# Masking the blocks that were not chosen: from bf16 products on TensorE to an addition on GpSimd

## The reference

```python
imp = jnp.einsum('bgrsc,cj->bsgj', p_cmp, overlap_matrix(ncmp, n_slc))
score = jnp.where(causal[:, None, :], jnp.where(forced[:, None, :], FORCE, imp), NEG)
_, idx = lax.top_k(score, topn)                       # 8 blocks per query and group
...
scs = jnp.einsum('bqgrd,bqgkd->bqgrk', qb, kg).astype(jnp.float32) * scale
scs = scs - slopes[None, None, :, :, None] * dist.astype(jnp.float32)
p = jax.nn.softmax(jnp.where(dist >= 0, scs, NEG), axis=-1)
return jnp.einsum('bqgrk,bqgkd->bqgrd', p.astype(vg.dtype), vg)
```

## Time and profile before

| what | value |
|---|---|
| median of 3 runs | 872.6 us (870.66 to 873.0) |
| span of the profiled execution, first to last instruction | 867.2 us |
| median less span | 5.4 us |
| TensorE / VectorE / ScalarE / GpSimd busy | 91% / 66% / 49% / 13% |
| `nsa_phase`, first to last instruction | 540.45 to about 762 us |
| mean granted TensorE clock | 0.961 |

### The profile page before, as it was taken

The page is one execution under the profiler, slowest core; times in us unless marked ns, Lnnn a source line. Parts: engine busy times, 40 slices in busy tenths (PEclk is TensorE's granted clock), DMA queues, the critical chain, the costliest instruction groups (busy, mean ns, idle before and its releaser), DMA issues. The chain is left out here.

```text
span 867.2 us, 16180 instructions
## 1 busy us (share of the span) xinstructions
PE 786.8 (91%) x6290; PEld 664.0 (77%) x6290; DVE 571.2 (66%) x1334; ACT 426.7 (49%) x966; POOL 113.7 (13%) x61
## 2 busy tenths in 40 slices
PE   4899999996988889877989998989998999989996
PEld 4899987685777767756868887778877888878885
DVE  6961111035789899847755997899998988943332
ACT  5631111113556565626743322778888888822221
POOL 0000000002000000002105421123110332132220
PEclk9999999998999999969998999899999999989999
DMA  7220125243232323134134431500001111034421
GB/s 293 103 86 38 37 98 154 77 112 111 67 104 68 104 67 98 55 92 134 49 87 137 122 86 41 146 2 1 3 2 51 50 51 50 2 122 146 146 98 48
DMA packets 31788, 72.34 MB, mean 83 GB/s; under 512 B 5088, under 2 KB 13664, under 8 KB 30688
## 3 DMA queue, kind: packets, MB, share of 16 engines
q1 hardware_dynamic: 31712, 71.31, 26.8%
HBM read 55.04 MB, written 16.25 MB: 82 GB/s over the span
## 5 line engine op out<-in xcount | busy, mean ns | idle before, releaser
L1645 ACT ACTIVATE n_probs<-n_probs,n_negated_max 128x640 f32<-128x640 f32 (+7 forms) x128 | 94.2, 736 | 28.4 <-DVE n_negated_max L1714 28.1
L1723 DVE SCALAR_TENSOR_TENSOR n_probsT_low<-n_turned,n_probsT_high 128x512 f16<-128x512 f32 (+3 forms) x192 | 94.4, 520 | 16.8 <-ACT n_probsT_high L1655 14.1
L706 PE MATMUL n_turned<-identity,n_probs 128*128 128x128 f32 x528 | 82.9, 281 | 6.3 <-ACT n_probs L1645 4.3
L1655 ACT ACTIVATE n_probsT_high<-n_turned 128x512 f16<-128x512 f32 (+3 forms) x192 | 80.7, 454 | 12.2 <-PE n_turned L706 11.8
L1817 PE MATMUL n_scores<-w_and_keys_high,stacks 128*128 128x256 f32 (+2 forms) x192 | 75.2, 392 | 5.5 <-DVE n_negated_max L1714 3.4
L706 PEld LDWEIGHTS n_turned<-identity,n_probs 128*128 128x128 f32 x528 | 59.6, 142 | 24.1 <-ACT n_probs L1645 16.4
L1818 PE MATMUL n_scores<-w_and_keys_low,stacks 128*128 128x256 f32 (+2 forms) x192 | 61.9, 333 | 0.0
L620 PE MATMUL nat<-stacks,xT_high 128*128 128x256 f32 (+1 forms) x192 | 56.1, 292 | 2.3 <-issue 2.2
L621 PE MATMUL nat<-stacks,xT_high 128*128 128x256 f32 (+1 forms) x192 | 55.2, 287 | 0.0
L622 PE MATMUL nat<-stacks,xT_low 128*128 128x256 f32 (+1 forms) x192 | 55.1, 287 | 0.0
L180 PE MATMUL a_projected<-xT_high,w_and_keys_high 128*128 128x512 f32 x128 | 52.3, 409 | 0.7 <-ACT staged L189 0.7
(11 more groups left out here) (263 smaller groups left out, 2177.3 us busy)
## 6 DMA issues: line engine op xcount, KB each, us to landing
w_raw<-in_w_feat SPq DMA_DIRECT2D x23, 512.0 KB, 3.9
features<-staged SPq DMA_DIRECT2D x30, 256.0 KB, 2.5
a_raw<-features SPq DMA_DIRECT2D x36, 128.0 KB, 2.7
s_raw<-features SPq DMA_DIRECT2D x18, 256.0 KB, 4.1
branches_b_c<-in_x SPq DMA_DIRECT2D x8, 512.0 KB, 6.2
silu_gates<-staged SPq DMA_DIRECT2D x16, 256.0 KB, 2.0
gatesT<-silu_gates SPq DMA_DIRECT2D x8, 512.0 KB, 4.8
keys_and_w_out_raw<-in_w_out SPq DMA_DIRECT2D x4, 1024.0 KB, 5.2
```

What stands on the lines that cost most here:

```text
L706: mm = nc.tensor.transpose(dst[:, j, :], src[:, c:c + P], ident[:, :])
L1645: nc.scalar.activation(pr[:, n % PS, 0:w], pr[:, n % PS, 0:w], ACT.Exp, scale=-1.0, bias=nmax[:, hb % 4, qt:qt + 1], accum_out=sums[:, hb ...
L1655: nc.scalar.activation(pth[:, g % GS, 0:k, :], tp[g % TS][:, 0:k, :], ACT.Copy, scale=PSCALE).then_inc(t_high, 1)
L1723: nc.vector.scalar_tensor_tensor(out=ptl[:, g % GS, 0:k, :], in0=tp[g % TS][:, 0:k, :], scalar=PSCALE, in1=pth[:, g % GS, 0:k, :], op0=ALU ...
```

## The change

The mask is no longer a product. `choose` writes -1e30 itself for a block that was not chosen (else 0), into a table `unsel` that outlives `cmp_phase`. In `nsa_phase` GpSimd adds it, each entry broadcast over the 64 keys of its block, to the distance table, once for each of the two head groups and four query tiles, into a new table `mb` of 3328 columns; the masked `add_bias` reads `mb` instead of `bf`. Gone are: the transposes and the cast at the end of `cmp_phase`, the memset of the old table, the load of `blocks` (512 KB) and its cast, the 64 products of L1822 (two for each of 32 masked units), and the wait of `a_squares` for the cast.

```diff
@@ choose, on VectorE in cmp_phase
-                nc.vector.tensor_tensor(unsel[:, g, :, 0:NSLC], left[:, :, :], imp[:, :, :],
-                                        ALU.is_equal).then_inc(chosen, 1)
-                dve.wait_ge(chosen, g + 1)
+                ch.link(nc.vector.tensor_scalar(unsel[:, g, :, :], left[:, :, :], -BIG / 2, NEG, ALU.is_gt, ALU.mult))
...
@@ ScalarE and TensorE at the end of cmp_phase
-            act.wait_ge(chosen_turned, 1)
-            nc.scalar.copy(unselT[:, :, :], tp[0][:, 0:KV, :]).then_inc(mask_ready, 1)
...
-            pe.wait_ge(chosen, KV)
-            for g in range(KV):
-                mm = nc.tensor.transpose(tp[0][:, g, :], unsel[:, g, :, :].rearrange("p t j -> p (t j)"), ident[:, :])
-            mm.then_inc(chosen_turned, 1)
...
@@ nsa_phase
+    MASKED = [qt for qt in QT_ORDER if qt >= SEL_T]
+    MASK_COLS = [(0, 640), (640, 1408), (1408, 2304), (2304, 3328)]
...
-            sp.dma_start(blk_in[:, :], blocks).then_inc(consts_in, 16)
...
-                if n == MASK_AT:
-                    act.wait_ge(consts_in, CONSTS)
-                    nc.scalar.copy(blk[:, :], blk_in[:, :]).then_inc(mask_ready, 1)
...
@@ add_bias, on VectorE
+                if br == 1 and qt >= SEL_T:
+                    dve.wait_ge(masked, SEL_T * (h // RC) + MASKED.index(qt) + 1)
+                    b = mb[:, MASK_COLS[qt - SEL_T][0]:MASK_COLS[qt - SEL_T][1]]
...
@@ GpSimd
+            def mask_biases(c):
+                for qt in MASKED:
+                    if c >= 1:
+                        pool.wait_ge(biased, GU * c - NT + QT_ORDER.index(qt) + 1)
+                    blocks, (at, end) = 2 * (qt + 1), MASK_COLS[qt - SEL_T]
+                    by_block = lambda t: t.rearrange("p (b k) -> p b k", b=blocks)
+                    nc.gpsimd.tensor_tensor(by_block(mb[:, at:end]), by_block(bf[:, S - (end - at):S]),
+                                            unsel[:, c, qt - SEL_T, 0:blocks].unsqueeze(2).broadcast_to([P, blocks, 64]),
+                                            ALU.add).then_inc(masked, 1)
+
             def a_squares(half):
-                pool.wait_ge(mask_ready, 1)
...
+            mask_biases(0)
             a_squares(0)
             a_squares(1)
...
+                if hb == GU // NT - 2:
+                    mask_biases(1)
...
@@ scores, on TensorE
-                if n == NT:
-                    pe.wait_ge(mask_ready, 1)
...
-                    mm = nc.tensor.matmul(out, q, kl[br][:, keys], start=False, stop=not masked)
-                if masked:
-                    rows = slice(32 * (qt - SEL_T), 32 * (qt - SEL_T + 1))
-                    for out, keys in parts:
-                        mm = nc.tensor.matmul(out, unselT[rows, c, :], blk[rows, keys], start=False, stop=True)
+                    mm = nc.tensor.matmul(out, q, kl[br][:, keys], start=False, stop=True)
```

More of the change, by code:

```diff
@@ L1246, in _, with cmp_phase @@
             values(UN - 1)
-def cmp_phase(nc, sig, feat_dram, gate_dram, w_feat, xh, xl, ring, stacks, yr, ident, kch, kcl, vc3, vscale, glog, unselT,
+def cmp_phase(nc, sig, feat_dram, gate_dram, w_feat, xh, xl, ring, stacks, yr, ident, kch, kcl, vc3, vscale, glog, unsel,
               dist_cmp, row_valid, force, keys_high, keys_low, win_bias, win_in, dist_win):
@@ L1287, in cmp_phase @@
         c_turned, c_high, c_low, c_valued, c_summed = sem("c_turned"), sem("c_high"), sem("c_low"), sem("c_valued"), sem("c_summed")
-        chosen, chosen_turned, mask_ready, chain = sem("s_chosen"), sem("s_chosen_turned"), sem("s_mask_ready"), sem("s_chain")
+        chain = sem("s_chain")
         fill = Filler(nc, sig, ring, w_feat, xh, xl, fb, FIRST_OF["cmp"], CHUNKS, feat_dram, gate_dram)
@@ L1444, in _ @@
                                                 vscale[:, 1, br:br + 1], None, ALU.mult))
-            ch.link(nc.vector.memset(unsel[:, :, :, :], 0.0))
             dve.wait_ge(const_in, 48)
@@ L1572, in nsa_phase @@
         small = sb("n_a_small", [P, 4], F32)
-        blk_in = sb("n_blocks_in", [P, S], F32)
-        blk = sb("n_blocks", [P, S], BF16)
+        squares = sb("n_a_squares", [P, S], F32)
+        mb = sb("n_bias_chosen", [P, MASK_COLS[-1][1]], F32)
         pr = sb("n_probs", [P, PS, S], F32)
@@ L1585, in nsa_phase @@
         raw_in = [sem(f"n_raw_in{i}") for i in range(2)]
-        consts_in, mask_ready = sem("n_consts_in"), sem("n_mask_ready")
+        consts_in, masked = sem("n_consts_in"), sem("n_bias_masked")
         stack_high, k_ready = sem("n_stack_high"), sem("n_keys_ready")
@@ L1690, in a_sums @@
                 cut = slice(NT // 2 * A_H * half, NT // 2 * A_H * (half + 1))
-                nc.vector.tensor_reduce(arms[:, cut], blk_in[:, :].rearrange("p (h d) -> p h d", d=HD), AX.X,
+                nc.vector.tensor_reduce(arms[:, cut], squares[:, :].rearrange("p (h d) -> p h d", d=HD), AX.X,
                                         ALU.add).then_inc(a_vector, 1)
@@ L1768, in a_squares @@
                 part = ya[:, NT // 2 * half:NT // 2 * (half + 1), :].rearrange("p t d -> p (t d)")
-                nc.gpsimd.tensor_tensor(blk_in[:, :], part, part, ALU.mult).then_inc(a_pool, 1)
+                nc.gpsimd.tensor_tensor(squares[:, :], part, part, ALU.mult).then_inc(a_pool, 1)
             def a_norm():
                 pool.wait_ge(a_vector, 3)
-                pool.wait_ge(consts_in, CONSTS)
+                pool.wait_ge(consts_in, 16)
                 nc.gpsimd.tensor_tensor(by_head, by_head, arms[:, :].unsqueeze(2).broadcast_to([P, NT * A_H, HD]),
@@ L1808, in scores @@
                     pe.wait_ge(biased, n - 1)
-                if n == NT:
-                    pe.wait_ge(mask_ready, 1)
                 q = qs[:, h, qt * P:(qt + 1) * P]
                 first = tiles[n][0]
-                masked = br == 1 and qt >= SEL_T
                 parts = [(sc[n % 2][:, at:at + w], slice(first * P + key, first * P + key + w))
@@ L2077, in decoder_trunk @@
             swa_phase(nc, sig, feat_dram, gate_dram, w_feat, xh, xl, ring, stacks, vbs, vscale, yr, ident, dist_swa, sinks)
-            cmp_phase(nc, sig, feat_dram, gate_dram, w_feat, xh, xl, ring, stacks, yr, ident, kch, kcl, vc3, vscale, glog, unselT,
+            cmp_phase(nc, sig, feat_dram, gate_dram, w_feat, xh, xl, ring, stacks, yr, ident, kch, kcl, vc3, vscale, glog, unsel,
                       dist_cmp, row_valid, force, keys_high, keys_low, win_bias, win_in, dist_win)
@@ L2082, in decoder_trunk @@
         gates = sb("gatesT", [P, 2, KT, P], F32)
-        nsa_phase(nc, feat_dram, gate_dram, stacks, vbs, vw, ya, yr, ident, vscale, glog, unselT, keys_high, keys_low, raw, wl, gates,
-                  lam_size, w_out, full_bias, win_bias, win_in, blocks, subln)
+        nsa_phase(nc, feat_dram, gate_dram, stacks, vbs, vw, ya, yr, ident, vscale, glog, unsel, keys_high, keys_low, raw, wl, gates,
+                  lam_size, w_out, full_bias, win_bias, win_in, subln)
         out_phase(nc, x, gate_dram, final_row, out, stacks, ya, yr, ident, raw, wl, gates)
@@ L2124, in _constants @@
     force = np.where(j > cur, NEG, np.where((j == 0) | (j == cur) | (j == cur - 1), -NEG, 0)).astype(f32)
-    blocks = np.zeros((SEL_T, 32, S), f32)
-    for b in range(NSLC):
-        blocks[:, b, 64 * b:64 * b + 64] = NEG
-    blocks = blocks.reshape(P, S)
     return {"identity": np.eye(P, dtype=f32), "dist_full": full, "dist_win": win, "dist_swa": swa, "dist_cmp": cmp,
-            "query_scale": scale, "row_valid": row_valid, "force": force, "blocks": blocks}
+            "query_scale": scale, "row_valid": row_valid, "force": force}
 def _slab(w, columns):
```

11 lines of the change are left out of this document (4 added, 7 removed).

## The result

The changed kernel takes 859.07 us (median of 4 executions, 857.47 to 860.71) where the kernel before, run beside it, takes 872.8 (870.66 to 873.93). The ratio is 0.9867, with a 95% interval of 0.983 to 0.9904.

What follows compares the result with a forecast made beforehand. VectorE was taken to set the pace in the masked parts, ScalarE and TensorE close behind. Span 867.2 - 3.7 (steady heads) - 1.3 (first head) + 1.5 (held-up VectorE) = 863.7, plus 5.4: 869.1 us; range 865.5 to 873.0.

Steps and rivals of the forecast that it cites:

- What bounds the phase: In nsa_phase's masked parts VectorE sets the pace, idle 1.22 of 13.72 us; products are worth only its waits, not 16.7 us.
- rival 3: TensorE is the hidden bound of masked parts; VectorE's idle time goes altogether, 8.3 us gained, 864.3 us; chance 0.10.
- The steady heads: Masked parts of seven heads: without mask products each is 0.53 us shorter, 3.7 us in all; tiles 5 and 4 nothing.
- The first head: Start of masking in nsa_phase: without ScalarE's block table cast and two mask waits, 1.3 us saved (0.8 to 1.65).
- The barrier: End of cmp_phase: removing transposes and cast gains nothing, as the last store covers them; 0.8 us at most.
- The additions: GpSimd's first four mask additions in nsa_phase take 1.89, 1.67, 1.46, 1.24 us, finished well before the first masked bias.
- What they hold up: Start of nsa_phase: GpSimd's additions block four small VectorE instructions, 2.9 us late, costing 1.5 us net (0 to 3.1).
- rival 1: Only the small instruction with two SBUF inputs waits for GpSimd, not one-element ones; net cost 0.5 us, 868.1 us; chance 0.20.
- The sum: Whole kernel: span 867.2 - 3.7 - 1.3 + 1.5 = 863.7, plus 5.4, gives 869.1 us, 0.4% faster.
- The 5.4 us: Whole kernel before: gap between profiled span 867.2 and the runs' median 872.6, taken as fixed and added to the span.

Runs made afterwards that it cites:

- e1: Kernel before without the 64 mask products, so no block is masked; transposes, cast, load and waits stay: 860.89 us, ratio 0.9898.
- e2: Kernel before with mask products for query tiles 7 and 6 only, tiles 5 and 4 unmasked: 867.68 us, ratio 0.9969.
- e3: Kernel before with mask products for query tiles 5 and 4 only, tiles 7 and 6 unmasked: 864.23 us, ratio 0.9924.
- e4: Kernel before without mask products, block table load and its cast; transposes and cast at the end of cmp_phase stay: 859.84 us, ratio 0.9876.
- e7: The changed kernel, unchanged, measured and profiled again: 859.76 us, ratio 0.9905.
- e11: Changed kernel plus a wait in out_phase: VectorE's w_out subtraction starts after GpSimd's first o_yT_low: 858.68 us, ratio 0.985.
- e8: The kernel before, unchanged, second profile: 868.45 us.
- e10: Kernel before plus a wait in out_phase: VectorE's w_out subtraction starts after GpSimd's first o_yT_low: 869.4 us, ratio 0.997.
- e5: Changed kernel plus a memset and four chained VectorE tensor_scalar on 1, 3, 2 and 4 elements during GpSimd's additions: 866.38 us in one execution.
- e9: The kernel before, unchanged, third profile: 871.86 us.
- e6: Changed kernel with ScalarE's three casts of w_out moved to GpSimd: 856.92 us, ratio 0.9859.
- e12: Changed kernel with w_out casts on GpSimd, and VectorE's w_out subtraction in out_phase waiting for GpSimd's first o_yT_low: 854.1 us, ratio 0.9793.

## Why the prediction was wrong

**What bounds the phase: right.** VectorE sets the pace, and the products were worth far less than their 16.7 us of records. In rival 3 TensorE sets it and VectorE's idle time goes altogether; in fact 0.59 of 1.22 us of a masked part is left.

**The steady heads: the mechanism right, the term mis-sized** (3.7 us forecast, 6.6 measured). Two mistakes, worth about 1.5 us each. First, "the bias that now starts at 614.13 can start ... 0.53 earlier" lets the products ahead of the second mask stand where they were, at 613.44, although the first wait gone moves them too: the two tiles are worth 0.33 + 0.42 = 0.75. (Even the bracketed waits, 0.25 and 0.34, are too short for this: they count from the previous record's end, and neighbouring records of VectorE overlap by some 0.08 us.) Second, "the masks of tiles 5 and 4 show no wait of VectorE ... I count them at nothing" looked at VectorE alone. ScalarE's list of waits for the kernel before had 11.1 us in 22 waits for transposes from 555 us on, and the forecast didn't use it; e1, e2 and e3 show that these two tiles were worth 1.3 to 1.7 us.

**The first head: right** (1.3 forecast, 1.7 measured: 0.15 + 1.14 + 0.42 at its three steps). The 0.15 is at the fifth bias, ahead of any mask or cast, where profiles of the kernel before alone differ by 0 to 0.24, so 1.56 are left, within the upper end of 1.65. Of the 1.14 the cast has 0.6, as forecast, and the mask 0.53 instead of 0.44.

**The barrier: right.** The last store is issued at 535.66 and the first bias starts 4.08 us later, as it did before (537.95 and 542.03), with the transposes and the cast gone; e4, which keeps both, has 4.07.

**The additions: right** in size (1.90, 1.69 and 1.47 us) and in place; no bias waits for them.

**What they hold up: wrong** (1.5 us forecast, 0.1 measured). The step that failed is "VectorE stands still until the GpSimd instruction in progress ends", put on all four small instructions from a row with 4 elements. On one element a tensor_scalar isn't held (0.15 us in the middle of an addition); only the instruction with two SBUF inputs is, by 0.23 us, which `add_bias(2)` had spare. This is rival 1's mechanism, which had a chance of 0.20 and charged 0.5; what reached the path is the 0.1 of `stack(1)`. In the sum below the 0.1 lies within the first head's measured 1.7.

**The sum.** These three errors make 2.9 + 0.4 + 1.5 = 4.8 us of span. The start 2.3 us earlier and the 0.9 in the last part were not forecast. Most of the first is there already at an instruction well ahead of `cmp_phase`'s code (L1184 at 392.73 before, 390.56 after, in a part that the change doesn't touch), and e7 starts late again, so in this profile it is largely luck; whether some of it is the change's stays open. The 0.9 is granted clock at the start of `out_phase`: 1.00 against 0.93 behind the first product. It comes back in e7 and e11 (108.9 and 109.1 us) against e8 (109.8), and in e4, but not in e1 (110.0); no run shows why. **The 5.4 us** between the span and the median was taken as fixed, and that was wrong: each execution's own time is its span + 1.8 us, so the profiled one took 869.0 and belongs with the lower group of the kernel before, the median to the upper. That makes the other 3.6 us of the 11.6 between 869.1 and the changed kernel's profiled 857.47.

**What the change itself is worth**, as far as shown, is less than the 13.7 us between the medians: 8.3 to 8.5 us in its own phase. Much of the rest goes with a different share of executions in the upper group, which some 4 us part from the lower one in both kernels: 21 of 32 of the kernel before (and 14 of the 17 beside e10), two of nine of the changed one. Whether the change itself makes the lower group more frequent stays open. With the order fixed, e10 and e11 are 10.4 us apart; the last part's 0.9 and the open 1.3 us at the start are of the size of what this leaves.

## What to carry to other kernels

Before counting removed work at nothing because the engine that sets the pace doesn't wait for it, read the waits of the engine that feeds this one: work in a shared queue delays what stands behind it. When a wait goes, move everything behind it before pricing the next. Compare a profiled execution's own time with the median before using the difference: if they differ, look for a second group of executions. And before two profiles are compared, line up their granted clocks and take a second profile of the same kernel: here such copies differ by 0.24 us at one bias, by 0.7 us in one stretch and by 3.3 us in the last part.

## What the runs showed of the hardware

**One element passes, two don't.** Under a GpSimd instruction on SBUF, VectorE's tensor_scalar took 0.15 us on one element, but on 3, 2 and 4 it lasted until the end of a GpSimd instruction (0.43, 1.40 and 1.18 us). A tensor_tensor with two SBUF inputs is held on one element too (0.39 us in the changed kernel, 1.55 in e5, against 0.16 alone).

The Trainium skill, "Vector Engine (DVE) Microarchitecture Reference", section 5.1, allows both ports to a one-source instruction with source and destination in SBUF if the count of its outermost dimension other than one is even, or odd with equal source and destination. For 2, 3 and 4 elements the runs agree. A single element has no such dimension, so the rule leaves it open; by e5 (0.15 us) it isn't held.

**GpSimd gets in between.** With GpSimd's instructions back to back, each held instruction of VectorE's chain took one GpSimd instruction: in e5's one profile four of them ended with four successive ones, and the first bias behind them was 4.4 us late.

**Two engines, one order, 1.5 us at least.** A VectorE subtraction of 2.29 us that starts 0.57 us before GpSimd's makes TensorE wait 2.67 us for GpSimd's result; with GpSimd 0.04 us ahead TensorE waits 0.22, and its first product comes 1.5 us earlier. Which of them wins follows TensorE's clock: in e8 the first two transposes ahead of them took 0.66 us together, in e9 0.41, and the slower ones gave the faster kernel. All eleven profiles without the added wait agree: 0.66 us and GpSimd first in seven (before, changed, e1, e2, e4, e7, e8), 0.41 and VectorE first in four (e3, e5, e6, e9).

**A stretch at half clock comes early or late.** In the eight profiles whose first two transposes of `out_phase` took 0.66 us (these seven and e11), the first forty products behind take 9.2 to 10.2 us; in the six with 0.41 (e10 and e12 too) they take 10.6 to 11.9. In e8 the granted clock is at half from 4.6 us behind the last bias until 3.1 us behind the first product, in e9 from 6.6 us until 6.5 us behind it. So e9's transposes ran at full clock and more of its products at half.

**GpSimd casts as fast as ScalarE.** In e12 and e6 the 128x2048 cast of w_out went to GpSimd, where it took as long as on ScalarE (1.90 us both).
